# VectorE adds the second v row of every batch in the last two blocks of the retrieval layer

## The reference, cut to what matters

```python
u = jnp.take(expert_u, idx, axis=0)
h = jax.nn.gelu(jnp.einsum('td,thkd->thk', xb, u))
wgt = (gate * h).astype(xb.dtype)
return jnp.einsum('thk,thkd->td', wgt, jnp.take(expert_v, idx, axis=0))
```

## Time and profile before

| | us |
|---|---|
| median of 3 runs | 3113.2 |
| profiled execution, its time | 3117.73 |
| its span | 3115.9 |
| TensorE matmul busy | 2639.8 |
| VectorE busy | 2295.4 |
| GpSimd busy | 1255.6 |
| ScalarE busy | 960.8 |

### The profile page before, as it was taken

How to read it: one execution, slowest core, us unless ns; L and a number is a source line. 1 busy time by engine, 2 the same in 40 slices (tenths; PEclk the granted TensorE clock), 3 DMA queues, 4 the chain that set the end, 5 groups by cost and what they waited for, 6 DMA issues and landing times.

```text
span 3115.9 us, 31174 instructions
## 1 busy us (share of the span) xinstructions
PE 2639.8 (85%) x8204; PEld 1433.9 (46%) x8204; DVE 2295.4 (74%) x4977; ACT 960.8 (31%) x3104; POOL 1255.6 (40%) x1060
## 2 busy tenths in 40 slices
PE   8879999999998888999999879889877776676675
PEld 7866676555544544544444436434332222222222
DVE  2478777888866676888887676788887877666666
ACT  2134414333332232332444221433322323222222
POOL 0123334343443434334344444434544444544542
PEclk9899999999999999999999999999999999889888
DMA  8999999999999999999999999999999999999996
GB/s 276 243 418 409 381 415 419 419 419 419 420 420 418 417 408 412 408 403 414 382 401 376 415 420 419 421 420 419 421 421 422 421 421 422 421 422 422 420 421 268
DMA packets 203656, 1255.16 MB, mean 403 GB/s; under 512 B 31101, under 2 KB 34765, under 8 KB 67921
## 3 DMA queue, kind: packets, MB, share of 16 engines
q0 software_dynamic: 152064, 1107.36, 86.2%
q1 hardware_dynamic: 48656, 139.92, 12.5%
q10 hardware_dynamic: 2760, 5.88, 0.5%
HBM read 1247.39 MB, written 5.79 MB: 402 GB/s over the span
## 4 chain that ended last, share of the span: by engine, by line
DMA 43%; PE 35%; DVE 14%; issue 4%; ACT 2%; DVEq 1%; POOL 1%; ACTq 0%; POOLq 0%
DMA ring<-in_uv,idx 37%; PE acc L1100 16%; PE wide L1081 11%; DVE ring L1379 6%; DMA wring<-in_uv,idx 3%; PE wide L1298 3%; DMA wring<-in_w_q 2%; DVE acc_v L1390 1%; PE wide L1269 1%; DVEq L1363 1%; PE wide L1197 1%; DMA bias<-in_uv,idx 1%; DMA wring<-in_w_a 1%; POOL ring L845 1%; PE wide L1179 1%
## 5 line engine op out<-in xcount | busy, mean ns | idle before, releaser
L845 POOL DMA_INDIRECT ring<-in_uv,idx x906 | 1071.8, 1183 | 1557.3 <-PE acc L1100 1024.5
L1100 PE MATMUL acc<-ring,diag 128*128 128x512 f32 (+1 forms) x2808 | 1372.0, 630 | 274.1 <-ACT diag L890 259.2
L1379 DVE CUSTOM_DVE_ANT_0 ring<-ring,xb 128x1024 f32<-128x1024 f32 x906 | 1095.6, 1224 | 460.4 <-DMA ring<-in_uv,idx 424.5
L1100 PEld LDWEIGHTS acc<-ring,diag 128*128 128x128 f32 (+1 forms) x2808 | 539.3, 199 | 976.5 <-issue 958.7
L876 ACT ACTIVATE hgelu<-hdot 128x2 f32<-128x2 f32 x528 | 107.2, 203 | 1716.8 <-DVE hdot L1379 1716.3
L1081 PE MATMUL wide<-xm,wring 128*128 128x256 f32 (+5 forms) x2352 | 606.8, 407 | 22.8 <-DMA wring<-in_w_q 21.9
L1081 PEld LDWEIGHTS wide<-xm,wring 128*128 128x128 f32 x2352 | 426.9, 196 | 216.4 <-issue 108.1
L890 ACT ACTIVATE diag<-ident,hw 128x128 f32<-128x128 f32 x813 | 293.7, 396 | 45.6 <-PE acc L1100 3.3
L1390 DVE SCALAR_TENSOR_TENSOR acc_v<-ring,hw,acc_v 128x1024 f32<-128x1024 f32 x204 | 262.1, 1285 | 36.6 <-ACT hw L879 16.3
L879 ACT ACTIVATE hw<-hgelu,gate 128x1 f32<-128x1 f32 x1056 | 254.1, 287 | 39.3 <-issue 3.5
L1298 PE MATMUL wide<-wring,big 128*128 128x256 f32 (+1 forms) x536 | 124.8, 379 | 0.0
(11 more groups left out here) (242 smaller groups left out, 2001.5 us busy)
## 6 DMA issues: line engine op xcount, KB each, us to landing
wring<-in_w_a SPq DMA_DIRECT2D x141, 512.0 KB, 7.9
wring<-in_w_q SPq DMA_DIRECT2D x64, 576.0 KB, 8.1
ring<-in_uv,idx POOLq DMA_INDIRECT x906, 20.8
ring<-in_w_a SPq DMA_DIRECT2D x27, 512.0 KB, 7.5
out_y_prompt<-xb ACTq DMA_DIRECT2D x7, 512.0 KB, 8.6
att<-in_ln_g SPq DMA_DIRECT2D x4, 512.0 KB, 11.9
att<-in_ln_b SPq DMA_DIRECT2D x4, 512.0 KB, 15.3
xm<-in_xT SPq DMA_DIRECT2D x1, 1536.0 KB, 10.8
```

The lines of the kernel that those rows point to most:

```text
L845: pool.indirect_dma_start(slot(s), None, uv, bass.IndirectOffsetOnAxis(ap=idx[:, n % LISTS, j:j + 1], axis=0))\
L1100: k = mm(acc[0:width, c * 512:(c + 1) * 512], diag[:, r % DIAGS, 0:width], slot(s)[:, D + c * 512:D + (c + 1) * 512], start=(s == first), ...
L1379: V.tensor_tensor_reduce(u, u, x, 1.0, 0.0, ALU.mult, ALU.add, hdot[:, k, j:j + 1])\
```

## The change

One condition in `plan_sums` (L387) gets a second part. `len(PEERS)` is 9, so `n >= 7` are the blocks 6 and 7.

```diff
             else:
                 on_dve = dve_done + 1.3 < pe_done + 1.8
-            if m == BATCH0[n + 1] - 1:
+            if m == BATCH0[n + 1] - 1 or n >= len(PEERS) - 2:
                 on_dve = True
```

## The result

Over 21 runs each the changed kernel takes 3117.56 us (3112.16 to 3124.1) and the kernel before 3112.3 (3109.28 to 3114.8). The ratio is 1.0018, with a 95% interval of 1.0012 to 1.0024: 5.3 us slower, just inside the 0.2% that the forecast called no change, and more than the 2.0 us it gave.

What follows compares the result with a forecast made beforehand. DMA transfers were taken to bound the kernel. Profiled, 3117.73 + 1.8 (reserve) + 0.2 (end) = 3119.7 us; carried to the median, 3113.2 + 2.0 = 3115.2 us, 0.06% more, range 3110.5 to 3121.5.

Steps and rivals of the forecast that it cites:

- What bounds: Blocks 6 and 7: transfers set the pace at 421 GB/s, 4.98 us a batch; VectorE and TensorE wait for data.
- The place: Block 6's batches 400 to 428: 41.8 us of added sums against 17.7 us of VectorE's waits for gathers.
- The lag: By batch 429 VectorE is 24.1 us behind the landings; 19.4 us if a sum costs only its busy 1.28 us.
- The reserve: Gathers' queueing, 27.8 less 5.5 = 22.3 us, hides the lag in block 6; beyond it transfers run dry once, 1.8 us.
- rival B: Block 6: the reserve holds, only the end's 0.2 us is left: 3113.4, or 3111.7 with the fetches; chance 0.38.
- rival A: The forecast: the reserve just runs out at the end of block 6's first 29 batches, 3115.2 us; chance 0.42.
- Rival C: Block 6's first 29 batches: transfers sag once landings take under 12.6 us; 8.9 us lost, 3122.3 or 3124.3; chance 0.16.
- TensorE's and GpSimd's side: Blocks 6 and 7: TensorE's 150 to 200 us saved gain nothing; GpSimd's wait for VectorE costs nothing beyond the release.
- The port rule: Two-input VectorE sums block GpSimd's SBUF reads, so an issue may start up to 1.28 us later; left out of the sum.
- The end: Last batches: the sum of batch 526 costs nothing; TensorE's last four records at 1.2 GHz up to +0.7 us, +0.2 taken.
- Its range: Whole kernel: from B with fetches less 1.5 us of scatter, 3110.5, up to most of C, 3121.5 us.

Runs made afterwards that it cites:

- before_again: The kernel before, unchanged, measured once more; ratio 0.9999 (0.9990-1.0008).
- spread_after: The changed kernel with block 7's retrieval spread over 56 batches in place of 36; ratio to the kernel before 1.0011 (1.0002-1.0019).
- tiles12_after: The changed kernel with 12 tiles in the ring in place of 14; ratio to the kernel before 1.0028 (1.0016-1.0039).
- dose22: The kernel before plus 22 added VectorE sums, in three of four batches of 400 to 428; ratio 1.0002 (0.9993-1.0011).
- tiles12_before: The kernel before with 12 tiles in the ring in place of 14; ratio 1.0006 (0.9998-1.0015).
- after_again: The changed kernel, unaltered, measured once more; ratio to the kernel before 1.0011 (1.0002-1.0020).
- first29: The kernel before plus 29 added VectorE sums, in batches 400 to 428 alone; ratio 1.0010 (1.0001-1.0019).
- idle_work29: The kernel before plus one sum-sized VectorE instruction in each of batches 400 to 428, freeing no tile and taking no TensorE slot; ratio 1.0003 (0.9994-1.0012).
- rest50: The kernel before plus the other 50 added sums, from batch 429 on, none in batches 400 to 428; ratio 0.9996 (0.9987-1.0005).
- every2nd: The kernel before plus 15 added VectorE sums, in every second batch of 400 to 428; ratio 1.0009 (1.0000-1.0018).
- short29: The kernel before plus 29 added sums in batches 400 to 428, each covering 32 of 1024 columns; ratio 1.0006 (0.9997-1.0014).

## Why the prediction was right, and what it had wrong

**What bounds.** Right. Wherever VectorE kept up, the rate in block 6 stood at 421 or 422 GB/s (2500 to 2640 us), whoever added the v rows. TensorE lost 316 matmul records (8204 to 7888) for nothing.

**The place.** Right. The loss sits in block 6's first 29 batches, where the retrieval leaves VectorE 17.7 us, and it comes from VectorE's time.

**The lag.** Forecast 24.1 us, at 1.44 us a sum; measured 19.4. All 17.7 us of waits were used and 19.4 us came on top: 37.1 us for 29 sums, 1.28 each. That is the lower bound of the prediction to the digit: a sum's busy time. The prediction gave the likely reason there, that part of a sum's drain falls where one stood already.

**The reserve: the term that failed.** The prediction let the transfers run dry only below 5.5 us to landing, the shortest seen, and priced 1.8 us. With the true lag of 19.4 us that rule gives nothing at all, rival B. That the forecast of 3115.2 came near is therefore luck in good part: a lag 4.7 us too long put a price where its own rule had none. By its own signs rival A is wrong, too. It allowed one dip of a few us near 2610 us and landings after 5 to 8 us; the rate was low from 2480 to 2640 us, and the landings took 10.8.

The runs show another law. The rate sags long before the landings get short: with the time to landing at 19 to 21 us it was 413 GB/s, at 16 to 18 us 362, and but for one recovery (418 from 2580 to 2600 us) it stayed low to 2640 us, though no gather landed in under 9.0 us. From 2500 to 2640 us the rate of 379 leaves out 140 x (1 - 379/421) = 14.0 us of transfers. The prediction also held that a gap in the transfers is never caught up, and that failed as well.

Only part of that is paid, and the end shows the rest. DMA from 3085 us to 3100 us in steps of 5, before and then after:

```profile
3085.00:3090.00 5.00, 1.95 (x4) 0.68 (x4) 3.36 (x5) 1.12 (x5) 0.00 (x0) 1.00 0.24 100
3090.00:3095.00 5.00, 4.57 (x7) 2.08 (x8) 2.84 (x5) 1.40 (x6) 0.00 (x0) 0.66 0.09 36
3095.00:3100.00 5.00, 2.37 (x6) 0.69 (x4) 3.43 (x5) 1.12 (x5) 0.00 (x0) 1.00 0.06 26
```
```profile
3085.00:3090.00 5.00, 3.37 (x6) 0.85 (x5) 3.77 (x6) 1.08 (x4) 0.00 (x0) 0.71 1.01 419
3090.00:3095.00 5.00, 2.00 (x5) 0.64 (x4) 3.42 (x6) 1.08 (x4) 0.00 (x0) 0.97 0.86 357
3095.00:3100.00 5.00, 3.11 (x5) 0.92 (x4) 3.21 (x6) 1.08 (x4) 0.00 (x0) 0.50 0.11 43
```

Before, the last 10 us or so run at 26 to 36 GB/s, and 421/16 is 26.3: most DMA engines have finished, and one, for a while two, are still at work while the dots keep waiting for them. The single packets in the traces say so directly: in before only two engines have work from 3087.9 us and one from 3092.0 to 3102.2; in the changed kernel the last one is alone for 4.8 us, from 3096.9 to 3101.7. Counted in full-rate time, before leaves out 5 x (3 - 162/421) = 13.1 us in these three rows and after 5 x (3 - 819/421) = 5.3, so 7.8 us come back; with 3080 to 3085 us (357 against 423 GB/s) 8.6. 14.0 - 8.6 = 5.4 us, and the stretch grew by 5.6.

**The engines stand apart, and the sag draws them together.** Behind its data every gather has one packet of 4 bytes on each of the 16 engines (16896 for 1056 gathers), and the last gather counts as landed 0.44 us after the last of them. So the number of these packets, divided by 16, tells how far the engines have come on the mean (the "mean engine" below), and the landings tell it of the slowest. Gathers issued and not yet done, on the mean over the window:

| kernel, window (us) | slowest engine | mean engine | GB/s |
|---|---|---|---|
| before_again, 2540-2560 | 10.5 | 6.1 | 422 |
| spread_after, 2540-2560 | 8.5 | 3.9 | 421 |
| after, 2540-2560 | 5.6 | 2.3 | 394 |
| after, 2640-2660 | 5.9 | 4.8 | 422 |
| tiles12_after, 2640-2660 | 4.8 | 4.2 | 420 |

The slowest engine's queue, which sets the time to landing, doesn't decide: 5.6 gathers go with 394 GB/s and 4.8 with 420. The mean engine's does. In all stretches of 20 us from 2460 to 2760 us, of all kernels whose trace has every landing (before and dose22 lack some), the rate was 415 GB/s or more where the mean engine had 3.0 gathers or more, and 402 or less where it had under 2.4. That is why a sag starts when the landings still look comfortable. It also isn't all lost: the dots wait for the slowest engine, and the others had only their lead to lose. From 2700 to 2780 us the mean engine is 5.3 gathers ahead of the slowest in before_again and 1.5 in the changed kernel.

With 2.49 us a gather the account closes to 0.5 us for every kernel with a sag whose trace has every landing, the one with 12 tiles too. It runs from 35 us ahead of the result of block 5 to 280 us behind it, against before_again (tiles12_after against tiles12_before), in us, each rounded:

| kernel | transfers left out | lead used up | what remains | dots 880 to 911 later by |
|---|---|---|---|---|
| after | 14.5 | 10.4 | 4.2 | 4.3 |
| after_again | 15.1 | 11.6 | 3.5 | 3.9 |
| first29 | 14.1 | 11.6 | 2.6 | 2.7 |
| idle_work29 | 11.9 | 9.7 | 2.3 | 2.5 |
| tiles12_after | 19.6 | 11.8 | 7.8 | 8.1 |

Two things stay open: why the engines stand apart at all, and why the slowest one, too, loses some us while it has gathers queued. The sag isn't only engines without work. From 2500 to 2640 us the DMA share fell by 4% (1.01 to 0.97) and the rate by 10%; the rest is packets that took longer. Of the 8 KB packets 386 of 6399 took over 400 ns, where before 7 of 7127 did and the usual one takes 309 to 319.

The Trainium skill (DMA: Bandwidth & Descriptors, Latency and other measured facts) states that two of the sixteen DMA engines are usually slower than the rest, with DMAs that GpSimd issues. The end of this trace, with two engines and then one at work, fits that; the trace doesn't name the engines.

**Rival C** had the right kind of mechanism, a sag well above 5.5 us to landing. Its price at a lag of 19.4 us would have been 19.4 - 15.2 = 4.2 us, near the 4.6 of block 6. With its threshold of 12.6 us that is partly luck, as the rate was down at 18 us already.

**TensorE's and GpSimd's side.** No cost, as said. The granted clock fell from 0.97 to 0.72 in the stretch 2500 to 2640 us, between levels of 1.2 and 2.4 GHz, without a trace in block 7's pace: 314.3 us in rest50 with the same 64 sums as the change and the clock at 0.74 from 2800 to 3080 us. The port rule weighed in the prediction leaves no mark either: from 2470 to 2612 us an issue of a gather into the ring took 1123 ns on the mean, where it took 1172 before.

**The end.** Forecast +0.2, up to +0.7. From the last dot to the second half of the result (second L1409) there are 5.56 us before, 6.45 after and 6.51 in after_again. Both have the last four records at the lower clock:

```profile
3104.84 3.70 PE L1100 MATMUL acc<-att,diag 128*128 128x512 f32 x4 [2.16 <-ACT diag L890]
```

They take 3.70 us in place of 1.88, as the prediction's clause had it. But rest50, with the same last batches, has 5.73 (its last four take 2.98 us), and every2nd, whose last batches are those of before, has 6.43, with 1.88 us for its last four and 6.23 for the eight ahead of them, 5.37 before; so 0.9 us is within what the same instructions do there from one execution to the next.

**Its range.** The lower end is a slip: 3111.7 less 1.5 is 3110.2, not 3110.5. Nothing hangs on it.

**Open: a step of about 0.95 us.** In every kernel but before and before_again the last dot comes 0.5 to 1.1 us later, against before, than the dot of slot 1020, and in most of them the second L1442 comes some 0.9 us later than the dot of slot 900. In every2nd and rest50 the dots of slots 900 to 927 stand within 0.03 us of those of before, and slot 928 is 0.93 and 0.99 us later. It doesn't last: by slot 940 it is gone but for 0.1 us, and it is back at the last dot. So up to 1.1 us of what a length in the table has over that of before is this step, and the dots of slots 900, 978 and 1020 are the better measure: 3.6, 3.6 and 4.6 us for the changed kernel, 3.1, 2.7 and 3.7 for after_again, 2.0 at all three for idle_work29, and 0.1 at most for rest50 and short29. The changed kernel, after_again, spread_after and tiles12_after have one more such microsecond between slots 978 and 1020; rest50, with the same sums in block 7, hasn't. I didn't find what decides where such a step falls.

## What to carry to other kernels

Before work is given to an engine with a low busy share, sum its waits in the stretch where the work will stand: VectorE was at 74% of the span and had 17.7 us to spare where 37 were put. In a ring of gathers the time from issue to landing is the slowest DMA engine's queue, so the usable reserve is smaller than that time less the shortest landing; look at the DMA rate near the first lag, and at how staggered the transfers end. When runs scatter by more than the effect, compare profiles between two marks around the change and not by their spans, and read more than one mark, as a single one can sit on a step.

## What the runs showed of the hardware

- The DMA rate of indirect gathers of 8 KB per partition held 421 GB/s with 22.7 us to landing (tiles12_before) and sagged to 362 with 16 to 18 us (after), in one kernel family; at 200 to 220 us it was 416 at 12.6. The time to landing alone doesn't tell whether the engines are fed: the rate went with what the mean engine had queued (3.0 gathers or more: at least 415 GB/s; under 2.4: at most 402).
- The 16 DMA engines run apart by several gathers: from 2700 to 2780 us the mean engine is 5.3 gathers, some 13 us, ahead of the slowest in before_again, and at the end of before one engine works alone for 10.2 us.
- 29 instructions scalar_tensor_tensor of 1.28 us, each behind a drain and most of them followed by other short work, cost VectorE 1.28 us each on the mean; between two dots one took 1.44.
- Dots that wait for landings repeat to 0.03 us over slots 900 to 927 between executions of different kernels, while the start of block 6 scatters over 8 us.
